# Differential heads of the Sample attention: which operand is loaded into TensorE and which one moves

## What is computed

```python
def _diff_attention(q, k, v, q_pos, k_pos, lam, lam_init, g_subln, bias_table):
    s = jnp.einsum('bqhcd,bshcd->bhcqs', q, k) * HEAD_DIM ** -0.5
    s = s + bias                                      # 4 heads, 2 halves each of 64 dims
    p = jax.nn.softmax(jnp.where(visible, s, -jnp.inf), axis=-1)
    p = p[:, :, 0] - lam * p[:, :, 1]
    o = jnp.einsum('bhqs,bshv->bqhv', p.astype(v.dtype), v)      # 128 values a head
    o = _rmsnorm(o, g_subln) * (1.0 - lam_init)       # per head
    return o.reshape(B, Tq, DIFF_WIDTH)
```

## Time and profile before

| | |
|---|---|
| runs, us | 3211.3, 2762.94, 2774.21 |
| median, us | 2774.21 |
| profiled execution, us | 2770.25 |
| its span, us | 2768.5 |
| mean granted clock of TensorE | 0.966 |
| TensorE busy (matmul) | 92% of the span |
| VectorE, ScalarE busy | 54%, 33% |
| Sample attention in the span, us | about 1312 to 1510 |

### The profile page before, as it was taken

One profiled execution on the slowest core, in us unless ns is written; L12 is line 12 of the kernel. 1 busy time (PEld: TensorE's weight loads), 2 busy tenths in 40 slices (PEclk: granted clock), 3 DMA queues, 4 the chain that ended last, 5 costly groups with the idle time before them and its releaser, 6 DMA issues. The chain is left out here.

```text
span 2768.5 us, 38260 instructions
## 1 busy us (share of the span) xinstructions
PE 2546.0 (92%) x14986; PEld 2246.1 (81%) x14986; DVE 1500.6 (54%) x3002; ACT 905.7 (33%) x1535; POOL 172.9 (6%) x259
## 2 busy tenths in 40 slices
PE   6999999998899999998798878888999989999999
PEld 5899999898677777797665866677778889999998
DVE  3544444544487766643443478877655435444444
ACT  2122222332355333432212366653334223222221
POOL 1000000232001100032000000100000000000000
PEclk9999999999899999999888989999999999999999
DMA  4332222443533432353532523332222242222221
GB/s 142 109 100 76 77 76 75 145 132 90 164 104 106 114 106 73 100 171 108 157 110 100 162 57 101 90 86 78 77 65 61 80 157 67 75 73 76 77 77 69
DMA packets 332210, 274.43 MB, mean 99 GB/s; under 512 B 30944, under 2 KB 300672, under 8 KB 331392
## 3 DMA queue, kind: packets, MB, share of 16 engines
q1 hardware_dynamic: 332032, 271.99, 33.0%
HBM read 226.89 MB, written 34.83 MB: 95 GB/s over the span
## 5 line engine op out<-in xcount | busy, mean ns | idle before, releaser
L1102 ACT ACTIVATE w_hi<-w_raw 128x2048 fp32r<-128x2048 f32 (+1 forms) x160 | 304.1, 1900 | 352.3 <-PE a_result L952 116.6
L1591 DVE TENSOR_TENSOR w_lo<-w_raw,w_hi 128x2048 fp32r<-128x2048 f32 (+1 forms) x160 | 364.6, 2279 | 40.9 <-ACT w_hi L1102 40.3
L927 PE MATMUL a_gate<-a_XTh,w_hi 128*128 128x320 f32 x352 | 111.8, 318 | 8.7 <-DVE a_XTl L1284 8.7
L893 PE MATMUL a_result<-w_hi,a_XTh 128*128 128x256 f32 (+1 forms) x400 | 114.2, 286 | 3.1 <-issue 1.5
L895 PE MATMUL a_result<-w_hi,a_XTl 128*128 128x256 f32 (+1 forms) x400 | 112.8, 282 | 0.0
L894 PE MATMUL a_result<-w_lo,a_XTh 128*128 128x256 f32 (+1 forms) x400 | 112.8, 282 | 0.0
L928 PE MATMUL a_gate<-a_XTl,w_hi 128*128 128x320 f32 x352 | 111.1, 316 | 0.0
L929 PE MATMUL a_gate<-a_XTh,w_lo 128*128 128x320 f32 x352 | 110.9, 315 | 0.0
L927 PE MATMUL a_up<-a_XTh,w_hi 128*128 128x320 f32 x352 | 109.1, 310 | 0.0
L927 PE MATMUL c_gate<-c_XTh,w_hi 128*128 128x320 f32 x352 | 108.8, 309 | 0.0
L927 PE MATMUL c_up<-c_XTh,w_hi 128*128 128x320 f32 x352 | 108.8, 309 | 0.0
(11 more groups left out here) (464 smaller groups left out, 7342.1 us busy)
## 6 DMA issues: line engine op xcount, KB each, us to landing
w_raw<-in_w_gate SPq DMA_DIRECT2D x88, 512.0 KB, 4.0
w_raw<-in_w_up SPq DMA_DIRECT2D x88, 512.0 KB, 5.3
w_raw<-in_w_down SPq DMA_DIRECT2D x44, 1024.0 KB, 5.0
w_raw<-in_w_in SPq DMA_DIRECT2D x18, 1024.0 KB, 5.4
w_raw<-in_w_out SPq DMA_DIRECT2D x8, 1024.0 KB, 8.5
shared<-in_cache_diff_k SPq DMA_DIRECT2D x8, 1024.0 KB, 5.3
s_v_in<-in_cache_diff_v SPq DMA_DIRECT2D x8, 1024.0 KB, 5.2
h_keys<-key_scr SPq DMA_DIRECT2D x4, 1024.0 KB, 6.1
```

Source lines behind the costliest of these rows:

```text
L893: pe.matmul(out, XTh[:, i, tok], hi[:, i], start=(i == 0), stop=False)
L927: pe.matmul(out, hi[:, i], XTh[:, i, tok], start=(i == 0), stop=False)
L1102: act.activation(w_hi[:, slot(c), 0:n], w_raw[:, slot(c), 0:n], ACT.Copy).then_inc(hi_split, 1)
L1591: dve.tensor_tensor(w_lo[:, slot(c), 0:n], w_raw[:, slot(c), 0:n], w_hi.bitcast(F32)[:, slot(c), 0:n], ALU.subtract).then_inc(lo_split, 1)
```

## The change

In `weigh` the two operands change places: the values are loaded and the probabilities move, so that a batch's result is 128 values x (4 heads x 16 frames) in bank 7. VectorE copies it to its place in `oT_d` (128 partitions, heads x batches x frames), without a transfer. In the third sparse unit's turn TensorE turns the four heads (`diff_turned`), which gives 128 rows (8 batches x 16 frames) x 512 in bank 7, and ScalarE's square and VectorE's scaling read them there. `gather`, `o_batch` and their semaphores go.

```diff
-        o_batch = used[0:S, DSA_HEADS * B * S + DIFF_HEADS * VD:DSA_HEADS * B * S + DIFF_HEADS * VD + 1024].rearrange("p (a n) -> p a n", a=2)
+        oT_d = used[:, DSA_HEADS * B * S + DIFF_HEADS * VD:2 * DSA_HEADS * B * S].rearrange("p (h b i) -> p h b i", h=DIFF_HEADS, i=S)
...
-                def gather(b):
-                    sp.wait_ge(batch_copied, b + 1)
-                    sp.dma_start(o_rows[b * S:(b + 1) * S, 0:512], o_batch[:, b % 2, :]).then_inc(gathered[b % 2], 16)
...
                         if b:
-                            pe.wait_ge(batch_copied, b)
+                            pe.wait_ge(oT_d_ready, b)
                         for h in range(DIFF_HEADS):
                             for k in range(KT + 1):
                                 rows = slice(0, P if k < KT else S)
-                                last = pe.matmul(bank(7)[0:S, h * VD:(h + 1) * VD], pT[rows, u % 2, k, h * S:(h + 1) * S],
-                                                 v_in[rows, b % 2, k, h * VD:(h + 1) * VD], start=(k == 0), stop=(k == KT))
+                                last = pe.matmul(bank(7)[:, h * S:(h + 1) * S], v_in[rows, b % 2, k, h * VD:(h + 1) * VD],
+                                                 pT[rows, u % 2, k, h * S:(h + 1) * S], start=(k == 0), stop=(k == KT))
...
+                    if u == B + 3:
+                        pe.wait_ge(oT_d_ready, B)
+                        for h in range(DIFF_HEADS):
+                            last = pe.transpose(bank(7)[:, h * VD:(h + 1) * VD], oT_d[:, h].rearrange("p b i -> p (b i)"), ident[:])
+                        last.then_inc(diff_turned, 1)
...
-                        for n in range(2):
-                            act.wait_ge(gathered[n], 16 * (B // 2))
-                        act.activation(o_square, o_rows[:, 0:512].rearrange("p (h n) -> p h n", h=DIFF_HEADS), ACT.Square
+                        act.wait_ge(diff_turned, 1)
+                        act.activation(o_square, bank(7).rearrange("p (h n) -> p h n", h=DIFF_HEADS), ACT.Square
...
-                        if u >= 5:
-                            dve.wait_ge(gathered[(u - 3) % 2], 16 * ((u - 3) // 2))
-                        dve.tensor_copy(o_batch[:, (u - 3) % 2], bank(7)[0:S, :]).then_inc(batch_copied, 1)
+                        dve.tensor_copy(oT_d[:, :, u - 3, :], bank(7)[:, 0:DIFF_HEADS * S].rearrange("p (h i) -> p h i", i=S)
+                                        ).then_inc(oT_d_ready, 1)
...
-                        order.link(dve.tensor_tensor(o, o, orstd[:].unsqueeze(2).to_broadcast([P, DIFF_HEADS, VD]), ALU.mult))
+                        order.link(dve.tensor_tensor(o, bank(7).rearrange("p (h v) -> p h v", v=VD),
+                                                     orstd[:].unsqueeze(2).to_broadcast([P, DIFF_HEADS, VD]), ALU.mult))
```

More of the change, by code:

```diff
@@ L1781, in sample_attention @@
         weighted = sem("sa_weighted")
-        batch_copied = sem("sa_batch_copied")
-        gathered = [sem(f"sa_gathered{n}") for n in range(2)]
+        oT_d_ready = sem("sa_oT_d_ready")
+        diff_turned = sem("sa_diff_turned")
         oT_s_ready = sem("sa_oT_s_ready")
@@ L1896, in _ @@
                     load_diff_v(b)
-                    gather(b - 2)
                 sp.wait_ge(block_turned, batch_blocks[B - 1][-1] + 1)
@@ L1901, in _ @@
                     sp.dma_start(shared[:, t * D:(t + 1) * D], o_scr[t * P:(t + 1) * P, :]).then_inc(rows_loaded, 16)
-                gather(B - 2)
-                gather(B - 1)
                 sp.wait_ge(onormed, 1)
```

## The result

The changed kernel takes 2809.59 us (median of four runs, 2807.78 to 2811.08). Against the kernel before it stands at 1.0152, 95% interval 1.0138 to 1.0166: about 42 us slower. The median that was known of the kernel before, 2774.21 us, stood on three runs with an outlier, and the fourth run on record, 8708.55 us, is another; in the 13 to 19 runs taken beside each group of experiments it is 2766 to 2768 us.

The account below looks back on a forecast made before the run. TensorE, busy 92% of the span, was taken as the bound. From 2770.25 us, +0.5 at unchanged clock (weigh 0, transposes +0.5) and +18 for the clock (+11 and +7) gave 2789 us, range 2760 to 2800.

Parts of the forecast that it names:

- Eight weigh steps at unchanged clock: Differential weigh in the Sample attention: 5.16 us a step against 5.17, 0 us together, between -8 and +7.
- moving less is worth nothing: Weigh records: loading 128 columns takes as long as moving 128 did, so fewer moving columns save nothing; 0.109 us a record.
- The three batches behind a wait: Sample attention: weigh wholly at 1.2 GHz and a slower score, 18.3 to 21.9 us less 8.8 paid already; +11.
- The other five weigh steps: Differential weigh steps paying nothing for the clock today: 1.4 us each, +7 us, bounds 0 to 23.
- should come late in a step: The clock's fall in the other five weigh steps, assumed late, hence priced at 1.4 us each.
- Transposes: Four added 128x128 transposes behind the third sparse unit's weigh: +0.5 us on TensorE.
- Copy, transfers, reads from the accumulator: Shorter VectorE copy, no gather transfers, ScalarE and VectorE reading the accumulator: beside TensorE's chain, so 0 us.
- the forecast's own upper bound: Top of the main forecast's own range, 2780 to 2807 us, where the clock falls more often; chance 0.48.
- weigh as it stands holds the clock but hardly wins it back: Weigh before the change: keeps full clock if begun there, stays at 0.50 for more than 6 us after a fall.
- no row of the waits has TensorE waiting for a transfer: Waits view around the Sample attention: TensorE waits for VectorE's turned-key copies, 6.5 us in three waits, never for a transfer.
- rival A: Weigh swap is a draw for the clock too, falling only behind the three waits: 2771 us, chance 0.34.
- Rival B: Full array width returns or keeps the clock in weigh behind the three waits, saving 8.8 us: 2762 us, chance 0.14.

Follow-up runs that it names:

- x1 to x3: The changed kernel with each weigh matmul moving 64, 32, or twice 64 columns instead of 16, loads unchanged: 2810.87, 2808.02 and 2794.02 us.
- x5: The kernel before without the eight gather transfers, SyncE signalling in their place (sample's group A output wrong): 2768.53 us, ratio 1.0000.
- x3: The changed kernel with the four heads' 64 columns moved twice in every weigh matmul, 128 loaded and 128 moving: 2794.02 us, ratio 1.0100.
- x4: The kernel before with 64 columns of probabilities loaded in every weigh matmul instead of 16 (sample's differential rows wrong): 2773.39 us, ratio 1.0021.
- x7: The kernel before with VectorE's copies of the turned keys ahead of the two key search rounds instead of between them: 2753.5 us, ratio 0.9940.
- x6: The changed kernel with a batch's 20 weigh matmuls put between the next score's matmuls: 2822.43 us, ratio 1.0191.

## Why the prediction failed, by its steps

The direction and the mechanism were as forecast: the clock falls in weigh steps that no wait precedes and comes back, mostly, in a score. The size was not: +42 us against the +19 of the forecast, outside its range of 2760 to 2800 us. The terms, from the profiled executions, start to start:

- **Eight weigh steps at unchanged clock, forecast 5.16 us each, 0 in sum.** In the step at 1470.37 us the clock fell at about 1474.6. What was left to 1476.44 is a fifth of a step at 1.2 GHz (1.84 of 9.41 us), so the first four fifths took 4.23 us, 5.3 us for a whole one, against 5.17. Nearly a draw, as said (some 0.8 us over eight steps). The reason given ("moving less is worth nothing") is too strong, as x1 to x3 show.
- **The three batches behind a wait, forecast +11.** Weigh 9.34, 9.41 and 9.41 against 6.75, 8.92 and 6.78 us: +5.7. Their scores, to L2012, 5.83, 5.19, 6.03 against 3.66, 4.56, 3.66: +5.2. Sum +10.9. That this meets the forecast is in part luck, as two errors cancel: a step wholly at 1.2 GHz costs 4.2 us more (9.41 against 5.17) and not 5.2, and the score behind it 1.5 to 2.4 us more and not 0.9 to 2.1, when both are taken from start to start.
- **The other five weigh steps, forecast +7, bounds 0 to 23.** This is the step that failed. Weigh 8.60, 6.49, 6.07, 9.41 and 6.71 us, 37.3 against 25.9: +11.4. The scores behind the first two, 6.61 and 5.63 against 3.66 each: +4.9. The sparse units' work behind the last three, 5.80, 6.11 and 6.11 against 3.09, 3.28 and 3.37: +8.3, and the first sparse weigh +0.7. Sum **+25.3**, above even the upper bound. I had taken that the fall "should come late in a step" and would cost part of one score; it came 1.0, 3.7 and 4.2 us after the start of three of the steps, and the other two began at 1.2 GHz already, of which the last had 2.4 GHz for 3.4 us in its middle; the scores behind the first two ran at 1.2 GHz for 5.9 of 6.6 and 4.1 of 5.6 us. And I had priced the score alone behind these steps. Behind the last three there stand sparse units, whose scores did not bring the clock back for 24 us (1474.6 to 1498.5).
- **Transposes, forecast +0.5:** 0.59. **Copy, transfers, reads from the accumulator, forecast 0:** x5 has the transfers at 1.0000.
- These terms make 36.8 of the 37.9 us by which the stage grew; the rest is in the turned probabilities (1.72 us instead of 1.16 for batch 2) and in 0.1 us a batch between L2022 and the first weigh matmul.

A second fault lay in the range: the forecast's own upper bound was 2807 us, and I cut it at 2800 on the strength of the chances. The row that would have told better was in front of me: a single weigh of 8.99 us with busy 1.70 of 1.70 at 0.50. A stream with 128 moving columns could stay at 1.2 GHz for 9 us, so the forecast had no ground to expect less of one with 16.

One reading of the rows was wrong as well: "weigh as it stands holds the clock but hardly wins it back". In two of the three batches behind a wait the weigh step of the kernel before did win it back, at about 1375.5 and 1440.3 us, some 3.5 us after the step began; only the 8.99 us step did not (columns as in the earlier trace rows):

```profile
1375.30:1377.00 1.70, 1.70 (x14) 0.93 (x13) 0.00 (x0) 0.00 (x0) 0.00 (x0) 0.96 0.00 0
1439.90:1441.60 1.70, 1.70 (x14) 1.08 (x13) 0.00 (x0) 0.00 (x0) 0.00 (x0) 0.88 0.00 0
```

The changed weigh lost this: its three steps behind the waits stayed at 1.2 GHz to their end. The prediction also says that no row of the waits has TensorE waiting for a transfer. One has, 5.0 us before L995, but it lies in stage `h`, which the window of that view takes in.

The Trainium skill, TensorE: Matmul & The Clock Gate, Part 1, was cited for a gate that goes by how busy the engine has been. Read simply it gave rival A, 2771 us. In the profile after the engine is busy in each of the rows at 0.50 above, so the measurement decides against that reading. The Trainium skill, same page, section "LDWEIGHTS (loading the stationary operand)", was cited for loads whose time goes by the columns and not by the rows. That fits: loads of 16 rows and of 128 rows are alike here (the two forms of L2036 load in 277 and 285 ns on average). The length does not: the shortest of these loads lasts 181 ns, and not the 107 ns that the prediction took as the page's estimate for 128 columns.

Rival A is out, as the clock looks nothing like before. Rival B's premise was tried apart in x4 and does not hold. The 8.8 us that it counted on could be had in another way: taking away the waits (x7) gave back these and the time of the waits.

## What to carry to other kernels

When one operand of a matmul has few columns, the choice of which one moves is not neutral even where the time of a step at full clock is: here the swap was nearly a draw, 5.3 against 5.2 us, and cost 42 us, nearly all of it through the clock. Read a long step at 1.2 GHz as a price for all that stands behind it, and ask what is there to bring the clock back, before pricing a change by its own records. And look for short waits ahead of thin work: taking 7.3 us in all from four short waits was worth 14.7 us here, and moving VectorE's copies ahead of the search gave more than every other variant.

## What was not expected of the hardware

- Movement of 16, 32 or 64 columns in a record behind a 128-column load left the clock equally low (mean 0.66, 0.64 and 0.65 in the stretch). With 128 it was kept in the five weigh steps without a wait in front, and in none of the three behind a wait did it come back before the score (x3). With 16 loaded and 128 moving columns it came back within the weigh step in two of three (the kernel before). Why the clock goes by this is not shown.
- The instructions of the change in a mixed order kept TensorE at 1.2 GHz for 100 us while it was busy 94% of the time (x6).
- At 2.4 GHz the 40 records of a step, with their eight changes of height, took 6.01 us with 128 loaded and 128 moving columns, 5.17 with 16 and 128, 5.50 with 64 and 128. The prompt's rows of 128 and 128 columns, without a change of height, take 0.112 us a record (L1027, 14 records from 1747.58 to 1749.14 us), 4.5 us for 40; so the changes of height may be where the wider load costs, which was not tested.
